# The second half of the output projection's weights on ScalarE's queue, in a two-layer attention and mixture-of-experts encoder

## The chip, the cores and the metric

The kernel runs on one core of a Trainium2 chip. The metric is the device time in microseconds (us) of one launch, as the median of several runs. Everything is float32.

## The reference, cut to what matters

The reference is an encoder of DEPTH = 2 layers over 256 tokens of width 1024. Each layer is attention (16 query heads and 4 key heads of 64; the first layer global with rotary positions, the second windowed with a bias and a sink) followed by a mixture of 16 experts.

```python
for i in range(DEPTH):
    h = rmsnorm(x, ln_mix[i])
    qkv = h @ w_qkv[i]                       # 1024 x 1536
    q, k, v = ...                            # head norms, rotary positions in layer 0
    o = global_attention(q, k, v) or window_attention(q, k, v, rel_bias, sinks)
    x = x + o @ w_o[i]                       # 1024 x 1024: the weights of this study
    x = x + hier_moe(rmsnorm(x, ln_ffn[i]), ...)   # w1, w3, w2 of 16 experts: 96 MB a layer
```

## The kernel before, in words

**Order of the work.** There is no scheduler: each of the five engines has its own program, written out by hand, and semaphores tie them. A layer goes: transposes of x (`turn_x`, line 1158), six groups of projection matmuls `qkv(g)` (line 1220; g = 0, 1 are keys and values, 2 to 5 the queries), then attention in eight slices (`scores` 1255, `turn_probs` 1276, `weigh` 1289), into whose gaps TensorE puts the last `qkv` groups and the output projection `project(n, ...)` (line 1307), then routing and four expert groups (up matmuls at 1462, down matmuls at 1474, scatter at 1444 and 1431).

**Weights and buffers.** The 48 units of expert weights of a layer (2 MB each, two transfers of 1 MB, line 337) stream through 11 buffers, `held`. Five of these are the slots of the tensor `attw`; in the attention stage `attw` holds w_qkv (slots 0 to 2) and w_o (slots 3 and 4, called `wo`), so w_o of layer 1 can be fetched only when the expert units in those slots are used up.

**Queues.** SyncE (SP) issues all the large transfers, in one order on one queue. In layer 0: x, four quarters of the k and v weights (314), two transfers of 2 MB of q weights (310), w_o (324), then held units 0, 1, 2, 3, 9 and 10. In layer 1 the same order stands behind the end of layer 0's expert stream, and the held units come after a flag that all engines read. ScalarE (ACT) issues six small transfers at the start (466 to 472) and none later. GpSimd (POOL) copies the bias rows to memory once (435) and fetches 16 bias tiles for layer 1's attention (450).

**w_o before.** `load_wo(L, a)` is called for a = 0, 1 and issues for each the half c = 0 into partitions 0 to 63 and the half c = 1 into partitions 64 to 127: four transfers of 1 MB a layer, each of 64 partitions with four rows of 4 KB. Each adds 16 to `wo_landed`; `project` waits for 64 a layer before its first matmul:

```python
if bs[0] == 0:
    pe.wait_ge(wo_landed, 64 * (L + 1))      # line 1298
```

**ScalarE around the two new places.** In layer 0, for g = 1, `square_heads(1)` (544), `inverse_head_rms(1)` (549, 551) and the copy of the bias rows (595) stand in a row, and the next is `square_heads(2)`, which waits for `qkv(2)`. In layer 1, three copies bring the last sums of the experts to x (672, 674, 677), then `square_x(1)` squares x (484) and makes the root of the mean square (487, 489). On VectorE `mean_square` (730) waits for the squares, and in layer 1 the copies of the transposed second tile of x (`copy_xt(1, 1)`, 767) stand behind it; `qkv(1)` needs the first of these.

Of the kernel before, what the change touches and what calls it, by code (L numbers as in the profile page):

```python
# [22 lines left out]
P = 128  # L23
# [5 lines left out]
HEADS, KV_HEADS, HD = 16, 4, 64  # L29
# [56 lines left out]
def encoder(nc, x, ln_mix, w_qkv, q_norm, k_norm, w_o, rel_bias, sinks, ln_ffn, w_group, w_expert,  # L86
            w1, w3, w2, table, spread, out):
    with ExitStack() as ctx:
# [3 lines left out]
        def sem(name):  # L92
            return ctx.enter_context(nc.semaphore(name))
# [47 lines left out]
        wo = attw[:, 3:5, :].rearrange("p u f -> p (u f)").rearrange("p (b f) -> p b f", b=KB)  # L141
# [50 lines left out]
        q_scale = stat[:, 63:95].rearrange("p (t h) -> p t h", t=TT)  # L192
        rc = stat[:, 119:127].rearrange("p (b h) -> p b h", b=4)
        mx, nb, sm, _, se, _, rs = (stat[:, 34 + 4 * n:38 + 4 * n].rearrange("p (b h) -> p b h", b=2) for n in range(7))


# [5 lines left out]
        wo_landed = sem("wo_landed")  # L202
# [70 lines left out]
        def sum_bank(tt, half):  # L273

            return (4, 2)[tt] + half
# [26 lines left out]
        def _(sp):  # L302
# [17 lines left out]
            def load_wo(L, a):  # L320

                wov = w_o[L].rearrange("(a c j d) f -> c d a j f", a=2, c=2, j=4)
                for c in range(2):
                    sp.dma_start(wo[HD * c:HD * c + HD, 4 * a:4 * a + 4, :], wov[c, :, a]).then_inc(wo_landed, 16)

            def unit_source(L, n):
                g, j = divmod(n, UNITS)
# [52 lines left out]
            for a in range(2):  # L380
                load_wo(0, a)
# [3 lines left out]
            for L in range(DEPTH):  # L385
# [15 lines left out]
                if L + 1 < DEPTH:  # L401
                    for u in range(3):
                        wait_used(L, 37 + u)
                        load_wqkv(L + 1, u)
                    wait_used(L, 41)
                    for a in range(2):
                        load_wo(L + 1, a)
# [57 lines left out]
        def _(act):  # L465
# [5 lines left out]
            act.dma_start(small_rows[:, 2 * P:SMALL], sinks).then_inc(small_landed, 16)  # L471
            act.dma_start(consts[:, P:TABLE], table[:, P:TABLE]).then_inc(table_landed, 16)

            def square_x(L):

                for tt in range(TT):
                    if L == 0:
                        act.wait_ge(x_landed[tt], 16)
                    else:
                        act.wait_ge(moe_out_dve, L)  # L480
                        act.wait_ge(moe_out_act, 3 * L)
                    if tt:
                        act.wait_ge(squared, TT * L + tt)
                    act.activation(square_dump, x_sb[:, tt, :], ACT.Square,
                                   accum_out=ssq[:, tt:tt + 1]).then_inc(squared, 1)
                act.wait_ge(ms_ready, L + 1)
                act.activation(log, ms, ACT.Ln).then_inc(ms_log, 1)
                act.wait_ge(ms_log, L + 1)
                act.activation(root, log, ACT.Exp, scale=-0.5).then_inc(root_ready, 1)
# [46 lines left out]
            for L in range(DEPTH):  # L536
                act.preload_act_table_set("natural_log_exp_and_others")
                square_x(L)
                def square_heads(g):
                    w = KV_HEADS * HD if g < 2 else 512  # L540
                    act.wait_ge(qkv_done, 6 * L + g + 1)
                    if 6 * L + g:
                        act.wait_ge(hms_ready, 6 * L + g)
                    act.activation(sq[:, 0:w], ps[:, g, 0:w], ACT.Square).then_inc(sq_done, 1)

                def inverse_head_rms(g):
                    nh = KV_HEADS if g < 2 else 8
                    act.wait_ge(hms_ready, 6 * L + g + 1)
                    act.activation(hl[:, 0:nh], hm[:, 0:nh], ACT.Ln).then_inc(hms_log, 1)
                    act.wait_ge(hms_log, 6 * L + g + 1)  # L550
                    act.activation(hr[:, 0:nh], hl[:, 0:nh], ACT.Exp, scale=-0.5).then_inc(hroot_ready, 1)

                def copy_k():
                    act.wait_ge(turned, 5 * L + 1)
                    act.copy(kT.rearrange("p a t -> p (a t)"), ps[:, 6, :]).then_inc(turn_copied, 1)

                def copy_q(n):

                    a, tt = divmod(n, 2)
                    act.wait_ge(turned, 5 * L + 2 + n)  # L560
                    act.copy(qT[:, a, tt].rearrange("p j q -> p (j q)"),
                             ps[:, (7, 6, 4, 5)[n], :]).then_inc(turn_copied, 1)

                def exps(u):
                    act.wait_ge(max_ready, DUOS * L + u + 1)
                    if u >= 4:
                        act.wait_ge(pt_done, DUOS * L + u - 3)
                    tt, h0 = duo_place(u)
                    for h in range(2):
                        src, scale = ((ps[:, u % 4, 256 * h:256 * h + 256], q_scale[:, tt, h0 + h:h0 + h + 1]) if L == 0 else  # L570
                                      (prob[:, u % 4, h, :], 1.0))
                        last = act.activation(prob[:, u % 4, h, :], src, ACT.Exp, bias=nb[:, u % 2, h:h + 1],  # L572
                                              scale=scale, accum_out=sm[:, u % 2, h:h + 1])
                    if L == 1:
                        for h in range(2):
                            last = act.activation(se[:, u % 2, h:h + 1], sink[:, h0 + h:h0 + h + 1], ACT.Exp, bias=nb[:, u % 2, h:h + 1])
                    last.then_inc(exp_done, 1)
# [10 lines left out]
                for g in range(4):  # L588
                    square_heads(g)
                    if g == 3:  # L590
                        copy_k()
                    inverse_head_rms(g)
                    if L == 0 and g == 1:
                        act.wait_ge(bias_made, 1)
                        act.copy(bias_rows, ps[0:HEADS, 3, 0:REL]).then_inc(bias_copied, 1)
                copy_q(0)
                exps(0)
                copy_q(1)
# [76 lines left out]
                if L + 1 < DEPTH:  # L675
                    act.wait_ge(main.scattered, GROUPS * (L + 1))
                    act.copy(x_sb[:, 1, 512:D], ps[:, sum_bank(1, 1), :]).then_inc(moe_out_act, 1)


        @block.vector  # L680
# [986 lines left out]
```

## Time and profile before

| | |
|---|---|
| median of 3 runs | 635.4 us (635.37 to 635.41) |
| span of the profiled execution | 634.3 us |
| TensorE busy | 620.9 us, 98% |
| VectorE, ScalarE, GpSimd busy | 180.1, 139.3, 53.3 us |
| mean granted TensorE clock | 0.998 |
| moved by DMA | 229.9 MB, mean 362 GB/s over the span |

The page gives the span of its own execution, from the first to the last instruction, and no other time of that execution; the table sets the runs' median beside it, and the 1.1 us between them lie outside the instructions. "Busy" of TensorE counts overlapping matmuls as one stretch. The idle time of the other engines costs nothing as long as TensorE does not wait for them. Names with a q (SPq, ACTq) are an engine's instruction sequencer, which issues the transfers: the time of such a row is how long issuing took, not how long the data took; "to landing" is the time from the start of the issue until the data was there.

### The profile page before, as it was taken

The numbers are of one execution on the slowest core, as the hardware profiler recorded it, in microseconds if no ns is written. First come the engines' busy times: TensorE is split into PE (matmuls) and PEld (weight loads), VectorE is DVE, ScalarE is ACT, GpSimd is POOL, SyncE is SP. The second block draws the span as 40 slices with busy tenths as digits, with TensorE's granted clock in tenths as the row PEclk, the third lists the DMA queues.
The fourth block names the chain that finished last, engine by engine and source line by source line (L and its number), as shares of the span: only waits on it lengthen the run. The fifth ranks groups of instructions, "written<-read, shape, count | busy, mean of one in ns | idle before, by whom it ended". The sixth has DMA issues, their size and how long they took to land.

```text
span 634.3 us, 10484 instructions
## 1 busy us (share of the span) xinstructions
PE 620.9 (98%) x4409; PEld 255.9 (40%) x4409; DVE 180.1 (28%) x609; ACT 139.3 (22%) x372; POOL 53.3 (8%) x61
## 2 busy tenths in 40 slices
PE   8999999999999999999999999999999999999996
PEld 5445544434324334333244454453343343343221
DVE  1665834412102102100133667343111021021011
ACT  2136642210000000000131677331100000000011
POOL 0005420000000000000010475000000000000000
PEclk9999999999999999999999999999999999999999
DMA  8999909699999999999999997697999999999993
GB/s 318 293 270 421 385 3 368 228 418 420 422 421 420 422 422 419 421 420 420 399 295 243 346 405 272 239 380 268 421 419 421 421 421 421 421 420 421 419 418 122
DMA packets 44759, 229.94 MB, mean 362 GB/s; under 512 B 8271, under 2 KB 8561, under 8 KB 21666
## 3 DMA queue, kind: packets, MB, share of 16 engines
q1 hardware_dynamic: 43068, 224.66, 90.7%
q0 software_dynamic: 1312, 4.23, 2.0%
q8 instruction: 37, 0.61, 0.4%
q10 hardware_dynamic: 326, 0.31, 0.2%
q14 instruction: 16, 0.13, 0.1%
HBM read 228.10 MB, written 1.08 MB: 361 GB/s over the span
## 4 chain that ended last, share of the span: by engine, by line
PE 91%; DVE 3%; ACT 2%; DMA 2%; issue 1%; POOL 0%; DVEq 0%; ACTq 0%
PE ps L1462 35%; PE ps L1474 18%; PE ps L1220 12%; PE ps L1307 8%; PE ps L1400 5%; PE ps L1431 3%; PE ps L1289 2%; PE ps L1255 2%; PE ps L1276 1%; ACT attw L572 1%; PE ps L1538 1%; PE ps L1444 1%; DMA ring<-bias_rows 1%; DMA x_sb<-in_x_dram 1%; DVE attw L872 1%
## 5 line engine op out<-in xcount | busy, mean ns | idle before, releaser
L1462 PE MATMUL ps<-attw,work 128*32 128x512 f32 x1216 | 140.1, 593 | 0.0
L1474 PE MATMUL ps<-ring,work 128*32 128x512 f32 x960 | 105.0, 593 | 0.5 <-ACT work L651 0.5
L1462 PE MATMUL ps<-ring,work 128*32 128x512 f32 x832 | 100.5, 594 | 0.0
L1220 PE MATMUL ps<-attw,work 128*128 128x512 f32 x192 | 87.4, 598 | 0.1
L1462 PEld LDWEIGHTS ps<-attw,work 128*32 128x32 f32 x1216 | 40.1, 110 | 89.1 <-issue 89.1
L1307 PE MATMUL ps<-attw,work 128*128 128x512 f32 x128 | 60.0, 602 | 0.7 <-issue 0.5
L1474 PEld LDWEIGHTS ps<-ring,work 128*32 128x32 f32 x960 | 30.3, 110 | 70.0 <-issue 68.3
L1025 DVE TENSOR_TENSOR work<-work,ps 128x256 f32<-128x256 f32 (+1 forms) x24 | 11.5, 508 | 156.0 <-PE ps L1462 156.0
L1462 PEld LDWEIGHTS ps<-ring,work 128*32 128x32 f32 x832 | 27.3, 110 | 57.6 <-issue 52.7
L1220 PEld LDWEIGHTS ps<-attw,work 128*128 128x128 f32 x192 | 34.6, 190 | 37.9 <-issue 36.9
L440 POOL TENSOR_SCALAR attw<-attw,stat 128x256 f32<-128x256 f32 x40 | 40.8, 1024 | 51.8 <-DVE stat L886 51.6
L450 POOL DMA_DIRECT2D ring<-bias_rows x16 | 11.9, 746 | 265.9 <-PE ps L1220 240.7
L651 ACT COPY work<-ps 128x512 f32<-128x512 f32 (+1 forms) x18 | 9.5, 539 | 110.6 <-PE ps L1538 110.6
L1400 PE MATMUL ps<-ropet,x_sb 128*128 128x128 f32 x256 | 33.5, 279 | 0.0
L1400 PEld LDWEIGHTS ps<-ropet,x_sb 128*128 128x128 f32 x256 | 30.4, 192 | 4.2 <-issue 2.5
L1307 PEld LDWEIGHTS ps<-attw,work 128*128 128x128 f32 x128 | 22.4, 190 | 22.4 <-issue 22.0
L1039 DVE COPY work<-ps 128x512 f32<-128x512 f32 x12 | 8.3, 692 | 75.2 <-PE ps L1474 75.2
L656 ACT COPY work<-ps 128x512 f32<-128x512 f32 x12 | 7.0, 585 | 92.5 <-PE ps L1474 92.5
L996 DVE TENSOR_TENSOR work<-ps,next_gains 128x512 f32<-128x512 f32 (+1 forms) x32 | 21.1, 658 | 18.9 <-PE ps L1400 18.8
L641 ACT COPY ropet<-ps 128x256 f32<-128x256 f32 x8 | 3.0, 372 | 90.7 <-PE ps L1508 90.7
L1431 PE MATMUL ps<-work,ropet 128*128 128x512 f32 x48 | 22.2, 605 | 0.0
L1276 PE MATMUL ps<-consts,attw 128*128 128x128 f32 x128 | 20.9, 281 | 1.2 <-POOL attw L440 0.7
(161 smaller groups left out, 459.9 us busy)
## 6 DMA issues: line engine op xcount, KB each, us to landing
ring<-in_w_dram SPq DMA_DIRECT2D x112, 1024.0 KB, 26.2
attw<-in_w_dram SPq DMA_DIRECT2D x80, 1024.0 KB, 20.2
attw<-in_w_qkv_dram SPq DMA_DIRECT2D x4, 2048.0 KB, 17.4
attw<-in_w_o_dram SPq DMA_DIRECT2D x8, 1024.0 KB, 22.9
attw<-in_w_qkv_dram SPq DMA_DIRECT2D x8, 512.0 KB, 11.0
ring<-bias_rows POOLq DMA_DIRECT2D x16, 256.0 KB, 7.2
x_sb<-in_x_dram SPq DMA_DIRECT2D x2, 512.0 KB, 7.0
out_dram<-x_sb SPq DMA_DIRECT2D x2, 512.0 KB, 4.5
```

The lines of the kernel that those rows point to most:

```text
L440: last = pool.tensor_scalar(prob[:, u % 4, h, :], prob[:, u % 4, h, :], rc[:, u % 4, h:h + 1], None, ALU.mult)
L450: pool.dma_start(bias_sb[b], tile).then_inc(bias_landed[b], 16)
L996: return dve.tensor_tensor(xg[:, ks, t, :], ps[:, bank, :].rearrange("p (k c) -> p k c", k=4)[:, part], next_gains[:, L, ks].unsqueeze(2). ...
L1220: last = pe.matmul(ps[:, g, :], xT[:, k, P * tt:P * tt + P], wqkv[part][:, k, :], start=(k == 0), stop=(k == KB - 1))
L1255: last = pe.matmul(ps[:, 2 * jj + c, 256 * h:256 * h + 256], qT[HD * c:HD * c + HD, a, tt, 2 * jj + h, :], kT[HD * c:HD * c + HD, a, :], s ...
L1276: last = pe.transpose(ps[:, 6, q0:q0 + P], prob[:, u % 4, h, P * t:P * t + P], order)
L1289: last = pe.matmul(ps[HD * c:HD * c + HD, 7, 256 * jj:256 * jj + 256], vv[:, t, kv:kv + HD], pT[v % 2][:, c, t, :], start=(t == 0), stop=( ...
L1307: last = pe.matmul(ps[:, (4, 5, 2, 3)[n], :], oT[:, b, P * tt:P * tt + P], wo[:, b, 512 * half:512 * half + 512], start=(b == 0), stop=(b ...
L1400: last = pe.matmul(ps[:, bank, P * k:P * k + P], x_sb[:, t, c:c + P], pg_flat[:, t, :], start=True, stop=True)
L1431: last = pe.matmul(ps[:, sum_bank(t, half), :], pcT[:, t, :], y_sb[:, half, t, :], start=False, stop=False, skip_group_check=True)
L1462: last = pe.matmul(ps[row:row + SLOTS, bank[t], :], xg[:, k, t, row:row + SLOTS], w[:, e, k % 4, :], start=(k == 0), stop=(k == KB - 1), t ...
L1474: last = pe.matmul(ps[row:row + SLOTS, bank[t], :], hT[t][:, k, row:row + SLOTS], w[:, e, k % 2, 512 * half:512 * half + 512], start=(k == ...
```

## The change

SP's `load_wo` issues only the half c = 0. A new function of ScalarE's program issues the two transfers of c = 1, with the same semaphore: in layer 0 behind the copy of the bias rows, for layer 1 behind ScalarE's last copy of layer 0.

```diff
@@ SP
             def load_wo(L, a):

                 wov = w_o[L].rearrange("(a c j d) f -> c d a j f", a=2, c=2, j=4)
-                for c in range(2):
-                    sp.dma_start(wo[HD * c:HD * c + HD, 4 * a:4 * a + 4, :], wov[c, :, a]).then_inc(wo_landed, 16)
+                sp.dma_start(wo[0:HD, 4 * a:4 * a + 4, :], wov[0, :, a]).then_inc(wo_landed, 16)
@@ ScalarE
+            def load_wo_second(L):
+
+                wov = w_o[L].rearrange("(a c j d) f -> c d a j f", a=2, c=2, j=4)
+                for a in range(2):
+                    act.dma_start(wo[HD:P, 4 * a:4 * a + 4, :], wov[1, :, a]).then_inc(wo_landed, 16)
+
@@ ScalarE, heads of layer L, group g
                     if L == 0 and g == 1:
                         act.wait_ge(bias_made, 1)
                         act.copy(bias_rows, ps[0:HEADS, 3, 0:REL]).then_inc(bias_copied, 1)
+                        load_wo_second(L)
@@ ScalarE, end of layer L
                 if L + 1 < DEPTH:
                     act.wait_ge(main.scattered, GROUPS * (L + 1))
                     act.copy(x_sb[:, 1, 512:D], ps[:, sum_bank(1, 1), :]).then_inc(moe_out_act, 1)
+                    load_wo_second(L + 1)
```

ScalarE's program in layer 0, from the head norms of group 1 to group 2; ps is PSUM, work a scratch tensor. Before:

```order
L544 ACTIVATE work<-ps 128x256 [waits hms_ready,qkv_done]
L549 ACTIVATE stat<-stat 128x4 [waits hms_ready]
L551 ACTIVATE stat<-stat 128x4 [waits hms_log]
L595 COPY ring<-ps 16x512 [waits bias_made]
L544 ACTIVATE work<-ps 128x512 [waits hms_ready,qkv_done]
```

And of the change, where the line numbers behind the edit are larger by 5:

```order
L549 ACTIVATE work<-ps 128x256 [waits hms_ready,qkv_done]
L554 ACTIVATE stat<-stat 128x4 [waits hms_ready]
L556 ACTIVATE stat<-stat 128x4 [waits hms_log]
L600 COPY ring<-ps 16x512 [waits bias_made]
L477 DMA attw<-in_w_o_dram 64x4x1024 x2
L549 ACTIVATE work<-ps 128x512 [waits hms_ready,qkv_done]
```

Two issues, which wait for nothing, stand now between the bias copy and the squares of group 2. At the end of layer 0 the same pair stands between ScalarE's last copy (677) and the table load of layer 1 (537).

SP's program where layer 1's weights are fetched, before:

```order
L314 DMA attw<-in_w_qkv_dram 128x2x512 [waits m_w13_used]
L314 DMA attw<-in_w_qkv_dram 128x2x512 x3
L310 DMA attw<-in_w_qkv_dram 128x8x512 [waits m_w13_used] x2
L324 DMA attw<-in_w_o_dram 64x4x1024 [waits m_w13_used]
L324 DMA attw<-in_w_o_dram 64x4x1024 x3
L296 TENSOR_LOAD flag [waits flag_ready]
```

And of the change:

```order
L314 DMA attw<-in_w_qkv_dram 128x2x512 [waits m_w13_used]
L314 DMA attw<-in_w_qkv_dram 128x2x512 x3
L310 DMA attw<-in_w_qkv_dram 128x8x512 [waits m_w13_used] x2
L323 DMA attw<-in_w_o_dram 64x4x1024 [waits m_w13_used]
L323 DMA attw<-in_w_o_dram 64x4x1024
L296 TENSOR_LOAD flag [waits flag_ready]
```

Two of four w_o issues are gone from SP; all that stood behind them, the flag and the held units, moves up by two.

## Rows read from the trace of the kernel before

**Rows 1.** The page: busy time of each engine, share of the span, instructions.

```profile
PE 620.9 (98%) x4409; PEld 255.9 (40%) x4409; DVE 180.1 (28%) x609; ACT 139.3 (22%) x372; POOL 53.3 (8%) x61
```

**Rows 2.** All waits of PE: who waited for whom, us in total, times, longest.

```profile
PE ps L1255 <- ACT attw L561: 1.4, 4, 0.6
...
PE ps L1158 <- DMA x_sb<-in_x_dram: 0.7, 1, 0.7
```

**Rows 3.** Sums by stretch: us, busy (count) of PE, PEld, DVE, ACT, POOL, clock, DMA share, GB/s.

```profile
29.00:44.00 15.00, 15.00 (x47) 7.09 (x46) 8.47 (x27) 2.98 (x8) 0.00 (x0) 1.00 1.02 222
44.00:79.00 35.00, 34.10 (x177) 18.68 (x175) 23.59 (x72) 23.88 (x72) 16.50 (x16) 1.00 1.01 408
79.00:95.00 16.00, 15.80 (x75) 7.95 (x76) 5.69 (x16) 7.36 (x20) 4.17 (x4) 1.00 0.03 4
...
325.00:355.00 30.00, 30.00 (x85) 13.91 (x84) 12.78 (x48) 6.19 (x21) 3.65 (x5) 1.00 1.03 234
...
385.00:395.00 10.00, 9.65 (x58) 5.26 (x56) 7.30 (x35) 8.58 (x32) 5.01 (x5) 1.00 0.73 241
```

**Rows 4.** SP's issues in order of time: start us, us, engine line, what, count.

```profile
17.87 1.31 SPq L324 DMA_DIRECT2D attw<-in_w_o_dram  x1
26.23 2.10 SPq L337 DMA_DIRECT2D ring<-in_w_dram  x1
28.38 4.03 SPq L337 DMA_DIRECT2D ring<-in_w_dram  x1
...
309.15 4.93 SPq L310 DMA_DIRECT2D attw<-in_w_qkv_dram  x1
314.12 5.41 SPq L324 DMA_DIRECT2D attw<-in_w_o_dram  x1
...
322.16 1.31 SPq L324 DMA_DIRECT2D attw<-in_w_o_dram  x1
```

**Rows 5.** Issues of window 17.9 to 18, 309.3 to 309.5 and 322.6 to 322.9: KB, us to landing.

```profile
attw<-in_w_o_dram SPq DMA_DIRECT2D x1, 1024.0 KB, 26.5
...
attw<-in_w_qkv_dram SPq DMA_DIRECT2D x1, 2048.0 KB, 23.7
...
attw<-in_w_o_dram SPq DMA_DIRECT2D x1, 1024.0 KB, 32.7
```

**Rows 6.** PE in order of time: the first use of w_o, and groups of layer 1.

```profile
38.53 0.60 PE L1240 MATMUL ps<-consts,attw 128*128 128x128 f32 x4
...
65.87 1.95 PE L1307 MATMUL ps<-attw,work 128*128 128x512 f32 x4 [0.25 <-issue]
...
323.50 17.33 PE L1220 MATMUL ps<-attw,work 128*128 128x512 f32 x40
348.41 2.74 PE L1220 MATMUL ps<-attw,work 128*128 128x512 f32 x6
...
375.83 1.95 PE L1307 MATMUL ps<-attw,work 128*128 128x512 f32 x4 [0.25 <-issue]
```

**Rows 7.** ACT in order of time, around its two new places; in brackets idle time before.

```profile
2.88 0.36 ACTq L472 DMA_DIRECT2D consts<-in_table_dram  x1
...
26.28 0.56 ACT L595 COPY ring<-ps 16x512 f32<-16x512 f32 x1
31.43 0.60 ACT L544 ACTIVATE work<-ps 128x512 f32<-128x512 f32 x1 [4.59 <-PE ps L1220]
...
318.68 1.28 ACT L537 ACT_TABLE_LOAD   x1
```

**Rows 8.** DVE in order of time, behind those two places.

```profile
34.43 0.69 DVE L815 TENSOR_TENSOR attw<-work 128x512 f32<-128x512 f32 x1
...
322.42 0.17 DVE L730 TENSOR_SCALAR stat<-stat 128x2 f32<-128x2 f32 x1 [2.46 <-ACT work L484]
323.26 1.29 DVE L767 TENSOR_TENSOR work<-ps,gains 128x512 f32<-128x512 f32 x2 [0.67 <-PE ps L1158]
```

**Rows 9.** One of DVE's waits in window 350 to 400 (layer 1's attention).

```profile
DVE attw L872 <- DMA ring<-bias_rows: 1.9, 2, 1.0
```

## The prediction

> **What bounds the kernel now.** I read the page's busy times first, then the waits of PE, then the sums by stretch with the DMA's rate, then the order of time on SP, PE, ACT and DVE around the edit. PE is busy 620.9 us of a span of 634.3 us [rows 1]: all that any change of transfers could give back is in the other 13.4 us, most of it start and end. The largest of PE's waits is 1.4 us in total, for the copies of q, and the only transfer in the list is x, with 0.7 us [rows 2]. No matmul waits for w_o. So the kernel is bound by PE's own work, and the question for this change is only whether it makes PE wait somewhere.
>
> **What the transfers of w_o do now.** The last of layer 0's four is issued at 17.87 us [rows 4] and lands 26.5 us later, at 44.4 us [rows 5]; `project` first wants it at 65.87 us [rows 6], 21.5 us later. In layer 1 the last is issued at 322.16 us and lands after 32.7 us, at 354.9 us; it is wanted at 375.83 us, 20.9 us later. While w_o moves, the engines' share is full, but the rate is 222 GB/s in layer 0 and 234 GB/s in layer 1 (there with other transfers among it), against 408 GB/s behind it in layer 0 [rows 3]. So transfers of 64 partitions, one half after the other, run at about half the rate. The Trainium skill's page "SBUF — State Buffer", section "Door 1: The DMA port swizzle", says that partitions 0 to 63 reach only 8 of 16 ports, worth about 218 GB/s; the 222 GB/s agree.
>
> **The change, part by part.**
>
> *Faster transfers.* If the two halves now run side by side, 4 MB could take 10.3 us (4.19 MB at 408 GB/s) instead of 18.9 us (at 222): a gain of up to 8.6 us of DMA time a layer; if they still take turns, 0. Neither moves the end. In layer 0 the DMA stands idle from 79 to 95 us, at 4 GB/s, because SP then waits for PE to free buffers; in layer 1 its share falls to 0.73 from 385 to 395 us [rows 3]. Earlier w_o only makes that pause longer. I take 0 us. The cover is that pause; without it the gain could reach the end only if PE waited for weights, and it does not [rows 2].
> The Trainium skill's page "DMA: Bandwidth & Descriptors", section "Rules for kernel authors", says of two transfers to disjoint partition halves: "Don't bother — they serialize". By that rule the DMA gain is 0 instead of up to 8.6 us, and the time of the kernel is the same 635.4 us by the one and by the other; no row of this trace has two halves in flight from two queues.
>
> *SP: two issues fewer a layer.* What stands behind them (held units 0 to 3, 9 and 10) is issued earlier. Those are wanted when the experts begin, long after the pause. 0 us.
>
> *Sharing: do layer 1's q weights come late?* ScalarE's pair goes out at about 319 us. The k and v weights are in use by then, but the second 2 MB of q weights, issued at 309.15 us, land only 23.7 us later, at 332.8 us [rows 4, 5]. ScalarE's 2 MB now move between them. All four w_o transfers took 354.9 - 332.8 = 22.1 us, so 2 MB take at most 11.1 us: the q weights land at the latest at 343.9 us. Their first matmul is at 348.41 us [rows 6]. 4.5 us are left. 0 us.
>
> *ScalarE's two issues.* This is the only cost that could reach PE. The rows give an issue into an empty queue 0.36 us on ACT [rows 7]; into a full one SP took 1.31 to 5.41 us [rows 4]. ScalarE's own queue has nothing in it at either place, so the nearest row is ACT's own: 2 x 0.36 = 0.7 us. That is also the lower bound, since the issue is added and nothing of ScalarE's is taken away; the upper is 10.8 us (2 x 5.41).
> Layer 0: the bias copy ends at 26.84 us and the next activation starts at 31.43 us, after 4.59 us of idle time [rows 7]. Behind that, VectorE has the query tile ready at 35.12 us (34.43 + 0.69) [rows 8], and PE turns it at 38.53 us [rows 6]: another 3.41 us. Room: 8.0 us. Price: 0.
> Layer 1: here a delay D of the squares moves VectorE's 730, which ends at 322.59 us, and behind it stand the copies of the second tile, 0.65 us each [rows 8]. `qkv(1)` starts when the first four of the 20 matmuls that begin at 323.50 us are done (40 instructions, two to a matmul of the code), each 17.33/20 = 0.87 us, so at 327.0 us [rows 6]. It needs 322.59 + D + 0.65 < 327.0, so D may be 3.7 us. With D = 0.7 us: 0.
> Sum: 0 us in both layers. Against the profiled span of 634.3 us the forecast is 634.3 us, and the median of the runs stands 1.1 us above that span, so 635.4 us.
>
> **The rivals.**
>
> *ScalarE's issues are held up by SP's (slower).* At both places SP is issuing into a full queue. If an issue on ACT has to wait until SP's is through, and then takes as long as SP's did at that moment, layer 0 costs the rest of SP's issue (28.33 - 26.84 = 1.49 us), then 2.10, SP's 4.03 and 2.10 us again: 9.7 us, 1.7 us over the room of 8.0. In layer 1: the rest of the 5.41 us issue that ends at 319.53 us (0.87 us from 318.66), then 1.3 us three times: 4.8 us, 1.1 us over the room of 3.7. Together 2.8 us: 638.2 us. It decides from 8.0 us in the one place or 3.7 us in the other. For it: SP's issues last up to 5.41 us [rows 4], and what one of them holds meanwhile the trace does not show. Against: the two have queues of their own, and ACT's issue at 2.88 us took 0.36 us [rows 7] while SP was issuing k and v weights (though into a queue that was not yet full). The Trainium skill's page "Perfetto Trace Analysis", section "DMA Instruction — HWDGE (DVE, Sync)", says that the descriptor generator is locked for exclusive use and that the profiled time of an issue holds the wait for the lock; by that rule it goes this way, and no run here shows it yet. Chance 0.13. A far tail, where ScalarE is held for as long as SP has anything to issue, would cost over 5 us: 0.02, inside the chance of slower.
>
> *Bias tiles come sooner (faster).* In layer 1's attention VectorE waits 1.9 us for bias tiles [rows 9], which share the DMA with w_o and what follows it. If the halves run side by side and the backlog is gone 8.6 us sooner, these waits could go, and with them at most 1.9 us of PE's: 633.5 us. Against: VectorE's wait is not PE's, and PE's waits name the copies of q, 1.4 us in total, before anything that hangs on the bias [rows 2]. Chance 0.07.
>
> *The halves still take turns.* The change then does not do what it says: two queues, one rate. The w_o lands as late as now and the kernel takes 635.4 us all the same. It is part of the forecast, not a price of its own; I give it 0.3 of the 0.78 below.
>
> **How the numbers follow.** Forecast, no change that can be measured: 0.78. Slower 0.15 (0.13 and 0.02), faster 0.07. A measurement of this kernel can tell about 0.2%, 1.3 us, from no change. The range of the forecast alone is 634.6 to 636.4 us. To hold 8 in 10 with some of the slower case, whose bounds are far apart, it goes up to its 638.2 us; below it takes half of the faster one, 634.4 us.
>
> **What would show it right or wrong.** In the changed profile: four ACTq rows on w_o, each under 0.6 us; the squares of group 2 in layer 0 still at about 31.4 us; the table load of layer 1 less than 1 us later; no wait of PE for w_o, and `project` still starting near 65.9 and 375.8 us. Side by side shows as over 350 GB/s in the stretch where w_o moves and a longer pause before 95 us; turns show as 222 GB/s again. It is wrong if ACTq rows of 2 us or more appear and PE's 1220 at about 327 us has a gap before it, or if the q weights land after 348 us.

## The result, and the profile after

The changed kernel takes 636.48 us (median of 13 runs, 635.42 to 637.19), the kernel before 635.57 us beside it. The ratio is 1.0015, with a 95% interval of 1.0008 to 1.0022: slower, by 0.15%. That is inside the bound of 0.2% that the prediction called no change, and inside its range, but the interval excludes 1, and the prediction had given 0 us. Two later comparisons gave 1.0007 (0.9998 to 1.0016) and 1.0008 (1.0000 to 1.0017). As means of the runs, the change costs 0.84, 0.67 and 0.46 us in the three; I speak of "some 0.7 us" below. Ratios and intervals here and below compare the executions one with another and are not the quotients of the two medians. Three executions far above all others (1079 us of the kernel before; 2271 and 2005 us of the change with the tail edit, below) are in the medians, but not in the means and ratios.

The profiled execution of the changed kernel happens to have the same span as the one of before, 634.3 us, and belongs to a run of 636.15 us. So 1.8 us lie outside the span. The later jobs show the same 1.8 us for the kernel before, so the 1.1 us of the prediction set an execution's span against the median of others.

ScalarE around its two new places in the changed kernel, in order of time (start, us, what; idle before in brackets), which answers to [rows 7]:

```profile
26.05 0.70 ACTq L477 DMA_DIRECT2D attw<-in_w_o_dram  x1
26.15 0.56 ACT L600 COPY ring<-ps 16x512 f32<-16x512 f32 x1
26.78 0.63 ACTq L477 DMA_DIRECT2D attw<-in_w_o_dram  x1
31.31 0.60 ACT L549 ACTIVATE work<-ps 128x512 f32<-128x512 f32 x1 [4.60 <-PE ps L1227]
...
317.52 0.62 ACTq L477 DMA_DIRECT2D attw<-in_w_o_dram  x1
...
318.18 0.63 ACTq L477 DMA_DIRECT2D attw<-in_w_o_dram  x1
318.84 1.28 ACT L542 ACT_TABLE_LOAD   x1 [0.29 <-issue]
```

SP was in one issue over the whole of the first pair:

```profile
22.98 6.16 SPq L336 DMA_DIRECT2D ring<-in_w_dram  x1
```

Each issue of ScalarE's takes 0.6 to 0.7 us, partly beside a copy of ScalarE's own engine; the squares in layer 0 keep their 4.60 us of idle time, and the table load is held by 0.29 us.

The sums by stretch of the changed kernel (us, busy and count of PE, PEld, DVE, ACT, POOL, then clock, DMA share, GB/s), which answer to [rows 3]:

```profile
29.00:44.00 15.00, 15.00 (x48) 7.07 (x47) 8.49 (x28) 2.98 (x8) 0.00 (x0) 1.00 1.02 265
44.00:79.00 35.00, 34.09 (x178) 18.75 (x176) 23.54 (x74) 23.92 (x72) 16.54 (x16) 1.00 1.01 380
79.00:95.00 16.00, 15.80 (x74) 7.89 (x76) 5.71 (x16) 7.37 (x20) 4.18 (x4) 1.00 0.15 30
...
325.00:355.00 30.00, 30.00 (x85) 13.94 (x84) 12.79 (x48) 6.31 (x21) 3.66 (x5) 1.00 1.03 243
...
385.00:395.00 10.00, 9.65 (x56) 5.16 (x56) 7.39 (x35) 8.56 (x31) 5.01 (x5) 1.00 0.76 253
```

Where w_o moves, the rate is 265 GB/s instead of 222, and behind it 380 instead of 408; the pause of layer 0 is shorter (share 0.15 instead of 0.03), not longer. SP's queue has two transfers fewer in front, so ScalarE's halves hardly meet SP's halves but the 128-partition transfers behind them, and slow those: 290 GB/s from 34 to 54 us. The w_o of layer 0 is therefore complete not sooner but later. Its last transfer, ScalarE's second of 26.78 us (issue, size, us to landing):

```profile
attw<-in_w_o_dram ACTq DMA_DIRECT2D x1, 1024.0 KB, 28.2
```

It lands at 55.0 us, where the kernel before had all of w_o at 44.4 us; `project` wants it near 65.8 us, so nothing waits. In layer 1 all of w_o is there at 354.7 us, as before (354.9 us).

How two queues share shows in the DMA view of 324 to 332 us, with packets, MB and share for each queue. The changed kernel:

```profile
q10 hardware_dynamic: 339, 1.32, 65.4%
q1 hardware_dynamic: 344, 0.70, 38.0%
```

The kernel before, same stretch:

```profile
q1 hardware_dynamic: 664, 1.81, 105.5%
```

q10 is ScalarE's queue, q1 SP's. The engines served the two in turn, packet by packet: 339 against 344. But ScalarE's packets hold 3.9 KB (a row of w_o) and SP's 2.0 KB (a row of q weights), so ScalarE got 1.32 of 2.02 MB and the q weights were down to 0.70 MB in 8 us, under 90 GB/s. The second 2 MB of q weights, issued at 309.32 us, show it (SP's issue, then size and us to landing):

```profile
attw<-in_w_qkv_dram SPq DMA_DIRECT2D x1, 2048.0 KB, 35.6
```

It was 23.7 us in [rows 5]. They land at 344.9 us, and PE starts on them at 348.30 us: 3.4 us of 15.5 are left. In this execution PE still had nothing to wait for there. Since the profile alone shows no loss, the loss had to be found by experiments.

### The profile page after: what moved, and what is told of

Same layout as the page of the kernel before. It is cut to its first block, busy times and chain, and to the rows that moved or that the text cites. A ratio compares the mean times of both kernels' runs of the same rounds, so it can differ in the third digit from the quotient of the medians.

```text
span 634.3 us, 10484 instructions
## 1 busy us (share of the span) xinstructions
PE 620.9 (98%) x4409; PEld 255.9 (40%) x4409; DVE 180.0 (28%) x609; ACT 139.4 (22%) x372; POOL 53.4 (8%) x61
## 4 chain that ended last, share of the span: by engine, by line
PE 91%; DVE 3%; ACT 2%; DMA 2%; issue 1%; POOL 0%; DVEq 0%; ACTq 0%
PE ps L1469 35%; PE ps L1481 18%; PE ps L1227 12%; PE ps L1314 8%; PE ps L1407 5%; PE ps L1438 3%; PE ps L1296 2%; PE ps L1262 2%; PE ps L1283 1%; ACT attw L577 1%; PE ps L1545 1%; PE ps L1451 1%; DMA ring<-bias_rows 1%; DMA consts<-in_table_dram 1%; DVE attw L879 1%
```

## The experiments

Two theories stood after the profile, beside one that looked outside the span. **Theory A**: the price lies outside the instructions. **Theory B**: it lies in the span, later split into **theory Q** (the q weights come after their use in some executions) and **theory T** (the backlog of transfers ends later, and with it the last bias tiles of layer 1's attention).

**The change again, and its two halves alone.** `f1_again` is the change unaltered.

> The change once more, unaltered, in the same job as the kernel before. Theory A: what it costs lies outside the instructions. Then the span stays within 0.3 us of the 634.3 us of before, and time minus span is near 1.8 us instead of the 1.1 us of before. Theory B: it lies in the span, because transfers from two queues hold each other up somewhere. Then the span grows by 0.5 to 1.5 us and time minus span is as in the kernel before.

636.26 us against 635.49 us (33 runs), ratio 1.0007 (0.9998 to 1.0016). The mean span is 634.34 us against 633.68 us for the kernel before, and 1.8 us are outside it in both. Theory A falls: all of the 0.67 us is in the span.

```diff
@@ f2_layer0_only, on the change
-                sp.dma_start(wo[0:HD, 4 * a:4 * a + 4, :], wov[0, :, a]).then_inc(wo_landed, 16)
+                for c in range(2 if L == 1 else 1):
+                    sp.dma_start(wo[HD * c:HD * c + HD, 4 * a:4 * a + 4, :], wov[c, :, a]).then_inc(wo_landed, 16)
-                    load_wo_second(L + 1)
@@ f3_layer1_only: the same with L == 0, and without load_wo_second(L)
```

> ScalarE issues the second half in layer 0 only; in layer 1 SP issues all four as before. Theory A (a price for a second queue that carries bulk, once a launch): the whole loss of the change, 0.9 us, or half of it if it goes by bytes. Theory B (a collision in layer 1, where bias tiles and q weights are under way): no loss, 635.5 us.

> ScalarE issues the second half in layer 1 only. Theory A: the whole loss, 0.9 us, or half of it by bytes. Theory B: the whole loss, and in the span; if layer 0's place is the cause, no loss here.

Layer 0 alone: 635.71 us, ratio 1.0001 (0.9992 to 1.0010). Layer 1 alone: 636.62 us, ratio 1.0015 (1.0006 to 1.0024). The loss is layer 1's; of layer 0 no loss can be measured, though 0.1% would fit in its interval. In layer 0 the mixing costs DMA time too (its pause is shorter, above), but nothing waits at its end.

**The issues without the bytes.** `f4_tiny` is the kernel before with a `spare` tensor, into which ScalarE fetches 2 KB twice at each of the two places.

```diff
+            def load_spare(L):
+                wov = w_o[L].rearrange("(a c j d) f -> c d a j f", a=2, c=2, j=4)
+                for a in range(2):
+                    act.dma_start(spare[:, 2 * L + a], wov[1, :, a, 0:2, 0:4]).then_inc(spare_landed, 16)
```

> The kernel before, with all of w_o on SP, and two issues of 2 KB each on ScalarE at each of the two places, into a spare tensor that nothing reads. Theory A with a price by issue: the loss of the change, 0.9 us. Theory A with a price by bytes or descriptors, and theory B: none, 635.5 us.

635.62 us, ratio 1.0000 (0.9991 to 1.0009). Four issues on ScalarE cost nothing that shows (0.09 us by the means): the price is one of bytes in the second queue.

**Q against T: ScalarE's pair later, and the dose doubled.** In `g1_late` the pair for layer 1 goes out behind the head norms of group 1, when the q weights have landed:

```diff
                         load_wo_second(L)
+                    if L and g == 1:
+                        load_wo_second(L)
...
-                    load_wo_second(L + 1)
```

> The change, with ScalarE's pair for layer 1 moved from the end of layer 0 to behind the head norms of group 1 (the same place as in layer 0), near 336 us, when the second 2 MB of q weights have landed. Theory Q (ScalarE's 2 MB slow the q weights, which land at 345 to 347 us in the profiles and in some executions after their use at 348.4 us): q weights land at about 333 us again and the loss is gone, under 0.2 us over the kernel before. Theory T (the backlog's end and with it the last bias tile comes later): the bytes and the queue are the same, so the loss of 0.7 to 1.0 us stays.

The q weights landed 22.7 us after their issue, as in the kernel before, but the kernel took 638.29 us against 635.99, ratio 1.0039 (1.0026 to 1.0052): neither 0 nor 0.7 us. Both theories missed it. ScalarE's 2 MB now mixed with the expert weights until 368 us, at 285 GB/s from 355 to 368 us, where the kernel before has 406 GB/s, and the bias tiles of POOL's queue were among them: those issued from 353 to 362 us took 10.5 to 12.5 us instead of 6.7 to 8.1. The waits of VectorE and of PE from 318 to 400 us in this kernel:

```profile
DVE attw L880 <- DMA ring<-bias_rows: 4.4, 4, 2.6
```

```profile
PE ps L1284 <- POOL attw L439: 2.5, 2, 2.1
```

VectorE waits 4.4 us for bias tiles instead of the 1.9 us of [rows 9], and PE waits 2.5 us instead of 0.7 for GpSimd, which works on what VectorE makes with them. This pointed at the bias tiles as the transfers on which the time hangs in layer 1.

In `g2_all4` ScalarE issues all four transfers of w_o for layer 1, and SP none:

```diff
-                    for a in range(2):
-                        load_wo(L + 1, a)
@@ load_wo_second
+                    for c in range(2 if L else 1):
+                        rows = slice(0, HD) if L and c == 0 else slice(HD, P)
+                        act.dma_start(wo[rows, 4 * a:4 * a + 4, :], wov[c if L else 1, :, a]).then_inc(wo_landed, 16)
```

> Double dose: ScalarE issues all four transfers of w_o for layer 1 at the end of layer 0, SP none. Theory Q: ScalarE's queue takes two thirds of the bytes for twice as long, the q weights land at 347 to 351 us, and PE waits for them at 348.4 us in the profile: 1.5 to 3 us over the kernel before. Theory T: 0.7 to 1.0 us as in the change, since the bytes and the end of the backlog are the same, and no wait at 348 us.

642.25 us, ratio 1.0093 (1.0080 to 1.0106): 6.3 us over the kernel before, twice the upper end of what theory Q expected. PE in order of time in this kernel:

```profile
353.05 5.46 PE L1227 MATMUL ps<-attw,work 128*128 128x512 f32 x6 [3.99 <-DMA attw<-in_w_qkv_dram]
```

The sums of the 8 us from 352 us on (us, PE, PEld, DVE, ACT, POOL, clock, share, GB/s):

```profile
352.00:360.00 8.00, 6.95 (x15) 2.99 (x16) 0.60 (x3) 0.00 (x0) 0.00 (x0) 0.57 1.01 268
```

The q weights now land after 43.2 us, at 352.9 us, and PE stands still for 3.99 us. The six instructions behind it take 5.46 us instead of 2.74 [rows 6], because the granted clock is 0.57 over these 8 us, mostly the lower of its two levels: 2.7 us more. So theory Q's mechanism is real at twice the dose, where wait and clock make 6.7 us in the profile. It does not say that the change itself reaches it.

**Q against T: the tail cleared.** In the kernel before, SP issues held unit 6 and the router's weights of layer 1 from 371 us on; they are the end of the backlog, beside which the last bias tiles move. Unit 6 is 2 MB; the router's weights are small, but in 1024 pieces of 16 bytes and 1024 of 64 bytes, and SP's issue of the second kind is its longest:

```profile
372.77 15.81 SPq L318 DMA_DIRECT2D wr<-in_w_expert_dram  x1
```

They land at 393.8 and 394.3 us. The tail edit issues them after the last maximum of attention. It is made on the kernel before (`g3_tail_before`) and on the change (`g4_tail_after`), and both again in another job (`h2_tail_before`, `h3_tail_after`), with the same edit on the layer 1 half (`h4_tail_layer1_only`) and the change once more (`h1_again`) beside them:

```diff
-                load_held(L, 6)
-                load_router(L)
+                if L == 0:
+                    load_held(L, 6)
+                    load_router(L)
...
                     sp.wait_ge(max_ready, DUOS * (L + 1))
+                    load_router(L)
+                    load_held(L, 6)
```

> The kernel before, with held unit 6 and the router's weights of layer 1 issued only after the last maximum of attention (near 395 us) instead of at 371 us. Theory T: the last bias tiles, issued at 384 and 387 us, have the DMA to themselves, and PE gains 0.3 to 0.8 us. Theory Q: nothing, 635.5 us, or less than 0.3 us.

> The same edit on the change. Theory T: level with the same edit on the kernel before, within 0.2 us, since the end of the backlog no longer matters. Theory Q: still 0.7 to 1.0 us above it, since the q weights come as late as in the change.

> The change a third time. Theory T (the mixing of the two queues in layer 1 wastes some DMA time, the backlog ends later, and the last bias tiles with it): 0.6 to 0.9 us over the kernel before, and in the profile the stretch from PE's last weighted slices to the end of attention is longer, not the stretch at the q weights. Theory Q (q weights late): a wait of PE before the sixth group's first matmul.

> The kernel before with unit 6 and the router's weights of layer 1 issued after the last maximum, a second time, now beside the change in one job. Theory T: 0.4 to 0.6 us under the kernel before. Theory Q: level with it.

> The change with the same edit, a second time. Theory T: level with the same edit on the kernel before (within 0.25 us), so the change costs nothing once the tail is clear. Theory Q: 0.6 to 0.9 us above it.

> The kernel in which ScalarE issues the second half in layer 1 only, which lost most (0.97 us by the means), with the tail edit. Theory T: level with the tail edit on the kernel before, within 0.25 us. Theory Q: 0.7 us or more above it.

Kernels of one job were measured beside the same executions of the kernel before; the runs whose names begin with f, g and h are jobs 1, 2 and 3.

| kernel | job | median us | before beside it | ratio, 95% interval |
|---|---|---|---|---|
| tail edit on before | 2 | 635.42 | 635.99 | 0.9993 (0.9984 to 1.0002) |
| tail edit on the change | 2 | 635.66 | 635.99 | 0.9990 (0.9981 to 0.9999) |
| the change | 3 | 636.29 | 635.69 | 1.0008 (1.0000 to 1.0017) |
| tail edit on before | 3 | 635.61 | 635.69 | 0.9996 (0.9987 to 1.0005) |
| tail edit on the change | 3 | 635.39 | 635.69 | 0.9994 (0.9985 to 1.0003) |
| tail edit on layer 1 only | 3 | 635.55 | 635.69 | 1.0001 (0.9992 to 1.0010) |

With the tail clear, the change is level with the kernel before: the ratios are 0.9990 and 0.9993 in one job, 0.9994 and 0.9996 in the other. By the means it is 0.14 and 0.20 us below, each plus or minus about 0.3 (two standard errors), so the 0.6 to 1.0 us that theory Q expected are excluded. Without the edit the change stands 0.0007 to 0.0015 above the kernel before, and 0.94 us (plus or minus 0.3) above the change with the edit in the same job. And the q weights come just as late with the tail edit (2.7 us before their use in the first of the two). So theory T holds, in that the loss hangs on what moves beside the last bias tiles, and theory Q does not reach the change. The edit takes away unit 6 and the router's many small pieces at once; which of the two slows the tiles was not separated. The tail edit on the change is the fastest version run, by the means; that it beats the kernel before is shown by one interval of two, and its size, 0.3 to 0.6 us, is hardly more than a measurement tells apart.

**Where it shows in the profiles.** The chain that ended last, of the kernel before, in the last slices of layer 1's attention (start, us, what):

```profile
386.77 6.88 DMA ring<-bias_rows
...
393.77 0.48 DVE attw L872
```

The last bias tile lies on the chain, with no slack, already before the change. The same place on PE, here in the kernel with layer 1's half alone (`f3_layer1_only`):

```profile
396.42 0.44 PE L1283 MATMUL ps<-consts,attw 128*128 128x128 f32 x2 [0.68 <-DVE attw L900]
397.21 0.44 PE L1283 MATMUL ps<-consts,attw 128*128 128x128 f32 x2 [0.35 <-POOL attw L440]
```

and in the tail edit on the kernel before (`h2_tail_before`), where the two waits are gone:

```profile
395.09 0.94 PE L1279 MATMUL ps<-consts,attw 128*128 128x128 f32 x4
395.95 1.99 PE L1310 MATMUL ps<-attw,work 128*128 128x512 f32 x4
```

I aligned the PE instructions of the twelve profiles that have no large wait by their number. The stretch from the q matmul that starts at 348.41 us in [rows 6] to the `project` matmul at 396.65 us differs by 1.2 us among them; all that lies before it differs by 0.4 us, all that lies behind it by 0.5 us:

| profile | GB/s, 318 to 355 us | last large transfer lands, us after that q matmul | last tile, us to landing | stretch us |
|---|---|---|---|---|
| before | 263 | 38.8 | 6.9 | 48.24 |
| layer 0 only | 264 | 38.6 | 6.5 | 47.88 |
| tiny | 255 | 39.6 | 7.5 | 48.79 |
| the change, three profiles | 259, 256, 250 | 38.6, 40.6, 39.6 | 6.9, 7.1, 7.5 | 48.25, 48.44, 48.79 |
| layer 1 only | 251 | 40.4 | 7.6 | 48.88 |
| tail on before, two | 269, 269 | 37.4, 37.2 | 3.6, 3.8 | 47.67, 47.65 |
| tail with ScalarE's pair in layer 1, three | 250, 251, 253 | 39.6, 40.7, 39.3 | 3.8, 3.8, 3.8 | 47.69, 47.67, 47.67 |

("Large" is the last expert transfer issued before 356 us.) Where ScalarE has its pair in layer 1, the rate from 318 to 355 us is 253 GB/s in the mean of seven profiles, where SP has all four, 264 GB/s in that of five: 0.4 MB less in these 37 us, which take 1.0 us at 404 GB/s. The last large transfer lands at 39.8 us in the seven, at 38.3 us in the five: 1.0 to 1.5 us of DMA time are lost to the mixing, by these means. The spread is as large: the tiny kernel, which has no bulk on ScalarE's queue, lies with 255 GB/s and 39.6 us among the seven. With a clear tail the later landing costs nothing, and all five stretches agree within 0.04 us, though with ScalarE's pair the last large transfer lands even later (39.3 to 40.7 us); without it the tile takes 6.5 to 7.6 us instead of 3.6 to 3.8 and the stretch is 0.2 to 1.2 us longer. One profile is no measure here: the profiles of the change and of before differ by 0.01 us in it, and the mean loss of some 0.7 us shows only over many runs.

## Why the prediction was wrong, point by point

**What bounds the kernel**: right, PE's own work; busy 620.9 us in both profiles.

**ScalarE's two issues, 0 us**: right. The issues took 0.6 to 0.7 us instead of 0.36 (the prediction had named under 0.6 as the sign), far from the upper bound of 5.41, and were hidden; the tiny transfers show it by themselves. The first rival, ScalarE held up by SP's issues for 2.8 us, did not come: ScalarE's two issues in layer 0 took 0.70 and 0.63 us within one issue of SP's that lasted 6.16 us (row above). The lock of which the Trainium skill's page "Perfetto Trace Analysis" speaks, in "DMA Instruction — HWDGE (DVE, Sync)", cannot have been held over all of SP's issue. That SP's long issues wait for room in SP's own queue, and hold up only SP, fits this but was not tested by itself.

**Faster transfers**: the cover was right in layer 0 and misread in layer 1. The text took "the halves side by side, up to 8.6 us earlier" and "in turn, as late as now" for the only two cases. The third happened: the halves of one queue mixed with whole transfers of the other, 265 GB/s where w_o moves but 380 behind, w_o of layer 0 was complete 10.6 us later instead of up to 8.6 us sooner, and the backlog ended later. "Earlier w_o only makes that pause longer" is the first half of the step that failed: the pause became shorter (share 0.15 instead of 0.03 from 79 to 95 us; in layer 1, from 385 to 395 us and without the tail edit, 0.76 to 0.89 in the four profiles with ScalarE's pair there and 0.73 to 0.81 in the three without).

**The pause of layer 1 as cover**: this is the other half, and where 0 us was wrong: the term for the transfers was put at nothing, and cost some 0.7 us. The share of 0.73 from 385 to 395 us was read as idle DMA with nobody waiting. A tile issued at 386.77 us was in flight in exactly this stretch and lay on the chain. The chain had the row; the prediction read PE's waits, where the same wait stands as 0.3 us each for VectorE and GpSimd, since PE names its last releaser and not the transfer behind it. That "PE's waits name the copies of q [...] before anything that hangs on the bias" was thus a wrong argument, and it was used only against a gain.

**Sharing, q weights at the latest at 343.9 us**: that they come later and still in time was right, the bound was not. They landed at 344.9 us in the change and at 346.7 us with layer 1's half alone. The bound put all of ScalarE's bytes in front of them and nothing else. But by 336 us ScalarE's pair was through (one of its packets is left in the 8 us behind), and from 336 to 344 us the rest of SP's queue shared the DMA with 0.63 MB of bias tiles, which in the kernel before moved behind the q weights. 3.4 us were left where 4.5 us were expected at least. The doubled dose shows how near that edge was.

**The Trainium skill's rule** ("DMA: Bandwidth & Descriptors", "Rules for kernel authors", on two transfers to disjoint halves: "Don't bother — they serialize"): the advice holds here, the change gains nothing. Whether two halves side by side would be faster stays open, since they hardly met: in layer 1 ScalarE's pair was through by 336 us, when SP's, which stood behind the q weights, had hardly begun, and in layer 0 they were together for under 2 us (214 GB/s from 32 to 34 us; behind that the whole transfers come in). No run issued them at the same moment.

**The second rival**, bias tiles sooner, had the right transfer and the wrong sign of the change in it. Its bound of 1.9 us was too large: with the waits for the last tiles gone, the gain over the kernel before is 0.2 to 0.6 us by the ratios of the tail edit, and one interval of four excludes 0.

**The numbers**: 0.15% lies in the band that got 0.78, but 636.5 us is just above the 634.6 to 636.4 us of the forecast alone. It is inside the range only because that was widened upward to 638.2 us for a rival that did not come, which is luck. The direction was missed because no term allowed for a cost below 1 us in either layer.

## What to carry to other kernels

A transfer moved to another engine's queue is not only issued elsewhere: it leaves the first-in, first-out order and shares the DMA engines packet by packet with what was ahead of it, so compare the packet sizes and list every transfer in flight until the backlog ends, the small ones first. A stretch in which the DMA is not full is cover only if no transfer on the chain is in it; look in the chain for DMA rows before calling DMA time free. For effects of 0.1%, undo the suspected wait on both kernels and compare the pairs, since one profile may show no difference at all.

## What the runs showed of the hardware that was not expected

- Two hardware queues were served one packet each in turn, 339 to 344 packets in 8 us, whatever their size, in this stretch: 1.32 MB for packets of 3.9 KB, 0.70 MB for those of 2.0 KB. The Trainium skill's page "DMA: Bandwidth & Descriptors", section "Queues, rings and completion order", says that each engine goes round the queues at packet granularity; the trace agrees, and its bytes show what unequal packets make of it.
- ScalarE's issues took 0.6 to 0.7 us while SP's, at the same time, lasted 6.16 us: SP's long issue did not hold up ScalarE's.
- A wait of PE of 3.99 us for weights cost about 2.7 us more behind it, in which the granted clock was down (0.57 over 8 us); in the kernel with ScalarE's pair later (`g1_late`) a PE wait of 2.1 us for the bias tiles went with 0.83 over 10 us.
- A bias tile of 256 KB from GpSimd's queue took 6.5 to 7.6 us beside the end of the backlog and 3.6 to 3.8 us with the tail edit.
- 64-partition transfers on one queue beside 128-partition ones on the other moved 290 GB/s together (layer 0 of the change, 34 to 54 us), against 222 for the halves alone and 408 for the whole ones alone.
